# A three-block transformer kernel on one core: the order of the first modulation units in its head

## The reference

```python
def rmsnorm(x, g):
    y = xf * lax.rsqrt(jnp.mean(xf * xf, axis=-1, keepdims=True) + EPS)
    return (y * g).astype(x.dtype)

def ada_modulation(cond, w, b):
    m = jax.nn.silu(cond) @ w + b          # 1024 -> 6 * 1024
    return jnp.split(m, 6, axis=-1)        # shift, scale, gate, shift, scale, gate

def modulate(x, g, shift, scale):
    return rmsnorm(x, g) * (1 + scale[..., None, :]) + shift[..., None, :]

# first_block, layer 0
h  = modulate(x,  norm_mix[0], sh1,  sc1)       # 256 tokens
hc = modulate(xc, norm_mix[0], csh1, csc1)      # 256 context tokens
q, k, v, r = jnp.split(h @ w_in, ...)           # gated linear attention
z = ((h @ w1) @ w2 + b)                         # its gate, of rank 16
```

## Times and profile before

| | us |
|---|---|
| runs | 1339.34, 1339.40, 1344.83 |
| median | 1339.4 |
| the profiled execution | 1338.25 |
| its span | 1336.3 |
| PE busy | 1309.8 (98%) |
| ACT busy | 684.6 (51%) |
| DVE busy | 583.3 (44%) |
| POOL busy | 707.5 (53%) |
| read from HBM | 208.15 MB, 157 GB/s over the span |

### The profile page before, as it was taken

The page is one execution under the profiler, slowest core; times in us unless marked ns, Lnnn a source line. Parts: engine busy times, 40 slices in busy tenths (PEclk is TensorE's granted clock), DMA queues, the critical chain, the costliest instruction groups (busy, mean ns, idle before and its releaser), DMA issues.

```text
span 1336.3 us, 22359 instructions
## 1 busy us (share of the span) xinstructions
PE 1309.8 (98%) x8256; PEld 1105.9 (83%) x8256; DVE 583.3 (44%) x1105; ACT 684.6 (51%) x1056; POOL 707.5 (53%) x307
## 2 busy tenths in 40 slices
PE   5999999999999999999999999999999999999999
PEld 1688788777888888888777757999999987999999
DVE  3423686235444443400036465455532485556620
ACT  4561236344444444422137745666665667766652
POOL 0432002352544444454435211698899775798897
PEclk8999999999999999999999999999999999999999
DMA  9533733471333322353534351666666541566664
GB/s 358 189 95 95 265 130 142 157 273 58 111 98 101 99 94 94 126 204 98 170 137 142 95 205 52 230 196 194 191 202 209 177 139 61 192 198 193 189 206 126
DMA packets 60133, 210.19 MB, mean 157 GB/s; under 512 B 6432, under 2 KB 9760, under 8 KB 59936
## 3 DMA queue, kind: packets, MB, share of 16 engines
q1 hardware_dynamic: 59632, 207.52, 47.1%
q10 hardware_dynamic: 432, 1.70, 0.3%
HBM read 208.15 MB, written 1.05 MB: 157 GB/s over the span
## 4 chain that ended last, share of the span: by engine, by line
PE 94%; DVE 2%; ACT 1%; DMA 1%; SPq 1%; issue 1%; ACTq 0%; DVEq 0%
PE ps L351 74%; PE ps L478 2%; PE ps L1121 2%; PE ps L406 1%; PE ps L1115 1%; PE ps L1107 1%; PE ps L388 1%; PE ps L398 1%; PE ps L1478 1%; DMA raw<-wstream 1%; PE ps L1457 1%; SPq L313 1%; PE ps L1460 1%; PE ps L1101 1%; PE ps L1438 1%
## 5 line engine op out<-in xcount | busy, mean ns | idle before, releaser
L340 POOL TENSOR_TENSOR wlo<-raw,whi 128x1024 fp32r<-128x1024 f32 x291 | 695.2, 2406 | 613.6 <-ACT whi L335 612.8
L335 ACT ACTIVATE whi<-raw 128x1024 fp32r<-128x1024 f32 x291 | 306.5, 1056 | 214.2 <-PE ps L351 145.0
L351 PE MATMUL ps<-Hhi_,whi 128*128 128x256 f32 (+1 forms) x1336 | 388.6, 319 | 0.0
L351 PE MATMUL ps<-Hlo_,whi 128*128 128x256 f32 (+1 forms) x1336 | 384.6, 316 | 0.0
L351 PEld LDWEIGHTS ps<-Hhi_,whi 128*128 128x128 f32 x1336 | 250.9, 188 | 22.7 <-issue 4.6
L351 PEld LDWEIGHTS ps<-Hlo_,whi 128*128 128x128 f32 x1336 | 251.0, 188 | 19.9 <-issue 1.9
L351 PE MATMUL ps<-Hhi_,wlo 128*128 128x256 f32 (+1 forms) x1336 | 231.7, 316 | 0.0
L351 PEld LDWEIGHTS ps<-Hhi_,wlo 128*128 128x128 f32 x1336 | 194.4, 188 | 18.1
L351 PE MATMUL ps<-hidhi,whi 128*128 128x256 f32 (+1 forms) x528 | 151.1, 315 | 0.0
L351 PE MATMUL ps<-hidlo,whi 128*128 128x256 f32 (+1 forms) x528 | 150.7, 314 | 0.0
L774 ACT ACTIVATE u<-ps,par 128x256 f32<-128x256 f32 (+1 forms) x132 | 83.8, 635 | 114.5 <-PE ps L351 100.6
(11 more groups left out here) (331 smaller groups left out, 1605.1 us busy)
## 6 DMA issues: line engine op xcount, KB each, us to landing
raw<-wstream SPq DMA_DIRECT2D x367, 512.0 KB, 3.6
Haside_lo<-wstream SPq DMA_DIRECT2D x8, 512.0 KB, 5.7
Haside_hi<-wstream SPq DMA_DIRECT2D x8, 512.0 KB, 9.3
Paside<-wstream SPq DMA_DIRECT2D x4, 512.0 KB, 5.0
XT<-x_t SPq DMA_DIRECT2D x1, 1024.0 KB, 10.4
XT<-ctx_t SPq DMA_DIRECT2D x1, 1024.0 KB, 12.5
memx<-mem_t ACTq DMA_DIRECT2D x1, 1024.0 KB, 5.4
out_t<-XT SPq DMA_DIRECT2D x1, 640.0 KB, 6.2
```

The source lines that it names most:

```text
L335: nc.scalar.activation(whi[:, n % RING, :], raw[:, r % RAWS, :], ACT.Copy).then_inc(S["hi_ready"], 1)
L340: nc.gpsimd.tensor_tensor(wlo[:, r, :], raw[:, r, :], whi[:, n % RING, :].bitcast(F32), ALU.subtract).then_inc(S["lo_ready"], 1)
L351: mm = nc.tensor.matmul(o, a, b, start=start, stop=stop)
```

## The change

The first norm's modulation is made in two batches of another make-up: units 0 and 2 (shift and scale of rows 0 to 3), and units 1 and 3 (of rows 4 to 7). Unit 2 is loaded right behind unit 0. Unit 3 leaves the ring and is loaded into the buffer of v. The products of units 1 and 3 stand together behind row 3 of the first tiles, and ACT's copy of their batch ahead of row 4. Beside that, ACT's table set that has both logarithm and exponential is named once in the head, ahead of the squares.

```diff
-QUEUE = [unit(0, 0), unit(0, 1), unit(0, 2), ("gate", "gate", 0, 1), ("gq", "gq", 0, 1), unit(0, 3), ("gq_", "gq", 1, 3)] + whole("gk", "gv")
+QUEUE = [unit(0, 0), unit(0, 2), ("gate", "gate", 0, 1), ("gq", "gq", 0, 1), unit(0, 1), ("gq_", "gq", 1, 3)] + whole("gk", "gv")
...
-ASIDE = [2, 3, 6, 7, 11]
+ASIDE = [(0, 3), (1, 2), (1, 3), (1, 6), (1, 7), (1, 11)]
...
-for _early, _unit in (("gate", "mod0_3"),):
+for _early, _unit in (("gate", "mod0_1"),):
...
-                if k < 2 and norm == "mix0":
-                    mod_products(pe, 0, 3, (2 * k, 2 * k + 1))
-                if k == 2 and norm == "mix0":
+                if k == 3 and norm == "mix0":
+                    mod_products(pe, 0, 1)
+                    mod_products(pe, 0, 3)
                     mod_turn(pe, 1)
...
-        BATCHES = [(0, 0, 3), (0, 3, 4), (0, 4, 8), (0, 8, 12), (1, 0, 4), (1, 4, 8), (1, 8, 11), (1, 11, 12)]
+        BATCHES = [(0, (0, 2)), (0, (1, 3)), (0, (4, 5, 6, 7)), (0, (8, 9, 10, 11)), (1, (0, 1, 2, 3)), (1, (4, 5, 6, 7)), (1, (8, 9, 10)), (1, (11,))]
...
             mod_products(pe, 0, 0)
-            mod_products(pe, 0, 1)
             norm_pe(pe, "mix0", TT)
             mod_products(pe, 0, 2)
...
             act.wait_ge(S["xin"], 32)
+            nc.scalar.preload_act_table_set(LN_EXP)
             for m in range(KD):
...
-                if t == "mix0" and k == 3:
+                if t == "mix0" and k == 4:
                     mod_row(act, 1)
...
             for n in range(RAWS, RAWS + LATE):
+                if n == RAW["mod0_1"]:
+                    load_aside(sp, (0, 3))
                 load_slot(sp, n)
             sp.dma_start(glac[:, :], gla_c).then_inc(S["glac"], 16)
```

More of the change, by code:

```diff
@@ L88 @@
     SRC += range(HOST[_host] + _first, HOST[_host] + _first + _count)
-ASIDE = [2, 3, 6, 7, 11]
-ASIDE_LOADED = {2: 128, 3: 128, 6: 256, 7: 256, 11: 320}
+ASIDE = [(0, 3), (1, 2), (1, 3), (1, 6), (1, 7), (1, 11)]
+ASIDE_LOADED = {(0, 3): 64, (1, 2): 192, (1, 3): 192, (1, 6): 320, (1, 7): 320, (1, 11): 384}
 ASIDE_SLOT = {}
 for _u in ASIDE:
-    _name, _host, _first, _count = unit(1, _u)
+    _name, _host, _first, _count = unit(*_u)
     ASIDE_SLOT[_u] = HOST[_host] + _first
@@ L315, in load_aside @@
         def load_aside(sp, u):
-            if u in (2, 3):
+            if u in ((1, 2), (1, 3)):
                 sp.wait_ge(S["slot_used"], used(START["go"] - 1))
-            elif u in (6, 7):
+            elif u in ((1, 6), (1, 7)):
                 sp.wait_ge(S["slot_used"], used(START["dn0"] - 1))
-            else:
+            elif u == (1, 11):
                 sp.wait_ge(S["a_o"], MH)
@@ L326, in aside @@
         def aside(u):
-            return {2: Haside_lo, 6: Haside_lo, 3: Haside_hi, 7: Haside_hi, 11: Paside}[u]
+            return {(0, 3): gv, (1, 2): Haside_lo, (1, 6): Haside_lo, (1, 3): Haside_hi, (1, 7): Haside_hi, (1, 11): Paside}[u]
         def hi_slot(act, n, i=0):
@@ L451, in alink @@
             nc.scalar.wait_ge(S["act_step"], counters["a"])
-        BATCHES = [(0, 0, 3), (0, 3, 4), (0, 4, 8), (0, 8, 12), (1, 0, 4), (1, 4, 8), (1, 8, 11), (1, 11, 12)]
+        BATCHES = [(0, (0, 2)), (0, (1, 3)), (0, (4, 5, 6, 7)), (0, (8, 9, 10, 11)), (1, (0, 1, 2, 3)), (1, (4, 5, 6, 7)), (1, (8, 9, 10)), (1, (11,))]
         MOD_BANK = {0: 2, 1: 3, 2: 7, 3: 7, 4: 7, 5: 2, 6: 7, 7: 7}
         def batch_of(layer, u):
-            return next(i for i, (L, a, b) in enumerate(BATCHES) if L == layer and a <= u < b)
+            return next(i for i, (L, units) in enumerate(BATCHES) if L == layer and u in units)
         def mod_products(pe, layer, u, slots=range(MOD_UNIT)):
             v, batch = u % 4, batch_of(layer, u)
-            first, last = u == BATCHES[batch][1], u == BATCHES[batch][2] - 1
+            first, last = u == BATCHES[batch][1][0], u == BATCHES[batch][1][-1]
             if first and batch in (3, 4, 7):
@@ L467, in mod_products @@
             for s in slots:
-                if layer == 1 and u in ASIDE:
-                    pe.wait_ge(S["aside_in"], ASIDE_LOADED[u])
-                    rows, signal = aside(u)[:, s, :], S["aside_used"]
+                if (layer, u) in ASIDE:
+                    pe.wait_ge(S["aside_in"], ASIDE_LOADED[layer, u])
+                    rows, signal = aside((layer, u))[:, s, :], S["aside_used"]
                 else:
@@ L482, in mod_row @@
         def mod_row(act, batch):
-            layer, _, end = BATCHES[batch]
-            if layer == 1 and end - 1 in ASIDE:
-                act.wait_ge(S["aside_used"], MOD_UNIT * (ASIDE.index(end - 1) + 1))
+            layer, units = BATCHES[batch]
+            end = units[-1] + 1
+            if (layer, end - 1) in ASIDE:
+                act.wait_ge(S["aside_used"], MOD_UNIT * (ASIDE.index((layer, end - 1)) + 1))
             else:
@@ L502, in mod_bias @@
             dve.wait_ge(S["mod_tr"], batch + 1)
-            L, a, b = BATCHES[batch]
+            L, units = BATCHES[batch]
+            a, b = units[0], units[0] + 1 if batch < 2 else units[-1] + 1
             va, n = a % 4, b - a
@@ L661, in norm_act @@
             if t in ("ffn0", "mix1"):
-                act.wait_ge(S["aside_used"], MOD_UNIT * (ASIDE.index(UNIT_AFTER[t][0]) + 1))
+                act.wait_ge(S["aside_used"], MOD_UNIT * (ASIDE.index((1, UNIT_AFTER[t][0])) + 1))
             for i, (k, halves) in enumerate(norm_items(t)):
-                if t == "mix0" and k == 3:
+                if t == "mix0" and k == 4:
                     mod_row(act, 1)
@@ L2316, in _ @@
                 for u in ((2, 3), (6, 7), (11,), ())[part_]:
-                    load_aside(sp, u)
+                    load_aside(sp, (1, u))
             sync_tail(sp)
```

## The result

| | before | changed |
|---|---|---|
| runs, us | 1339.13 to 1344.83 | 1355.85 to 1357.87 |
| median | 1339.37 | 1356.54 |
| ratio, 95% interval | | 1.0125 (1.0105 to 1.0145) |
| the profiled execution | 1338.25 | 1357.15 |
| its span | 1336.3 | 1355.2 |

The changed kernel is slower by 17.2 us, inside the range given (1348.5 to 1357), 3.7 above the point forecast (+13.4).

The account below looks back on a forecast made before the run. It took a chain of waits in the head, then PE, without a gap from 52 to 130 us, as the bound. Terms 1.1 + 4.9 + 6.1 + 1.3 = 13.4 on the median 1339.4 gave 1352.8 us, range 1348.5 to 1357.

Parts of the forecast that it names:

- rival 1: Wait ahead of row 4: PE's clock falls a third time, costing 1.3 to 1.7, total 1354.3; chance 0.29.
- Term A: Head, up to the first row: PE wakes late at low clock, ACT copies batch 0 at 29.9; +1.1, from -0.2 to +2.7.
- 28.06: Head: forecast end of PE's low clock, 2.56 of work after the norm's sum starts at 25.50.
- Term B: Between rows 3 and 4: units 1 and 3 and the chain behind them stand in the open; +4.9, from 4.5 to 6.6.
- Term C: End of first tiles: `glac` and `w2` wait on SP's queue behind two blocked slots; +6.1, from +5.0 to +6.6.
- Term D: Behind the wait for `w2`: PE works 2.56 at half pace; +1.3, from 0.9 to 1.7.
- The removed loads: Eight table loads on ACT, 10.3 in all, said to bring nothing when removed.
- rival 3: ACT's table loads on the path: 1342.5, or 1331.5 with a drain per load; chance 0.02 each.
- the prediction's signs: Listed checks per term, among them last row's products ending at 56.5 and `w2` products starting at 62.8.

Follow-up runs that it names:

- e_tables_only: The kernel before with only ACT's table set named in the head, ahead of the squares; 1339.16 us, ratio 1.0003.
- e_unit2_ahead: The changed kernel with unit 2's products on PE ahead of the norm's sum, nothing else; 1352.34 us, ratio 1.0096.
- e_run_head: The changed kernel with 24 products of no use on PE between unit 0 and the norm's sum; 1353.56 us.
- e_glac_early: The changed kernel with glac and w2 issued by SP ahead of the two slots that wait for the first tiles; 1346.86 us, ratio 1.0055.
- e_spread: The changed kernel with unit 3 in place of three idle products ahead of row 0 and unit 1 halved into the steps of rows 0 and 1; 1351.74 us.
- e_run_rows: The changed kernel with 5 products of no use on PE behind the turn of units 1 and 3, ahead of row 4; 1354.2 us.
- e_run_tail: The changed kernel with 14 products of no use on PE ahead of its wait for w2; 1357.05 us.
- e_before_w2_late: The kernel before with glac and w2 issued by SP four slots later, behind slots 20 and 21; 1352.85 us, ratio 1.0091.
- e_best: The changed kernel with glac and w2 issued early, unit 2 ahead of the sum, units 1 and 3 spread, table set named before the input wait; 1341.42 us.
- e_best2: As e_best, but row 0 directly behind four idle products, unit 3 in row 0's step, unit 1 halved into those of rows 1 and 2; 1340.27 us.
- e_run_all: The changed kernel with products of no use in three PE gaps: 24 ahead of the sum, 5 ahead of row 4, 17 ahead of w2; 1352.75 us.

## Why the prediction was right, point by point

- **The direction and the range held**, the range partly by luck. All four terms are there, beside them only rival 1 came, and nothing behind 157 us moved. But the median stands 0.5 below the top of the range, and that top was made for rival 1 with the upper ends of A and C, while here D too went beyond its own (2.5 against 1.7). With the 18.9 of the profiled executions in place of the 17.2 of the medians, 1358.3, the result would lie above it.
- **Term A**, +1.1 forecast, +2.5 measured in the profiled execution. The mechanism is right (the moved load cancels but for 0.33 at most, by the first stage of e_tables_only; the late waking of PE is the cost, as e_unit2_ahead and e_run_head show). The step that was mis-sized is "28.06": the low clock did not end 2.56 after the start of work but 6.1 after it (to 31.5). In e_glac_early it ended at 28.5, with a first stage of 12.61, so +1.3; in the four kernels that keep this head (e_glac_early, e_spread, e_run_rows, e_run_tail) the stage was +1.3 to +1.6, near the forecast. The 2.7 given as the upper end was about the price of this execution. One record of a change is no price: before, it could have been read only that 2.56 is a length that occurred.
- **Term B**, +4.9 forecast, and +5.07 measured in the second stage, all of which e_spread gives back (17.9 in every other kernel that keeps the place, 13.1 in e_spread and in those built on the kernel before).
- **Rival 1**, the third fall of the clock, got 0.29 and 1.3 to 1.7. It came true in the profile, and cost 2.26, with 6.06 of work at 0.50. In e_glac_early, where that stage is 8.52, it cost 0.99. The argument against it, that gaps of 0.97 and 1.15 had left the clock alone, said nothing on one of 2.46; the row for a gap of 2.0 did, and should have weighed more. No gap length is a rule, though: one of 2.45 in e_run_head left the clock at 1.00.
- **Term C**, +6.1 forecast, +6.72 measured. SP's order was read rightly from the order of instructions. The first slot was there for ACT 3.6 after SP's signal (59.12 to 62.69), as forecast; the second slot and the small transfers behind it took 4.5 and not 3.9, which is the 0.6. In the other profiles with this wait the stage is 7.1 to 8.2 long, so 5.8 to 6.9 more than before, around the forecast.
- **Term D**, +1.3 forecast, +2.50 measured, up to 3.58 in e_before_w2_late. The same mis-sized step as in A: half of 5.3 of work at low clock, and not half of 2.56.
- **The removed loads** brought nothing, as forecast (e_tables_only), and rival 3 falls with them. On the drain that rival 3 priced: in the rows of e_tables_only the first square starts 0.01 after the load's end, so no drain is to be seen here either.

In the profiled execution the sum missed by 5.5 (18.9 and not 13.4): 1.4 in A, 2.3 by rival 1, 1.2 in D, so 4.9 of it by the clock, and 0.6 in C and 0.2 in B, less 0.1 for the earlier input. That execution is 0.6 above the median of its kernel and the one of before 1.1 below its own, so the medians show 3.7 of it. One number among the prediction's signs does not follow from its own sum: the last row's products end at 49.62 in the kernel before (49.01 + 0.61), and 6.0 later is 55.6, not 56.5. Nothing rests on it.

## What to carry to other kernels

A transfer that waits on an in-order queue holds up every one behind it: when the stream is re-ordered, ask for each small transfer behind it who is now released later, and issue constants ahead of the first slot that waits for late work. Work taken out of a gap of PE can cost twice, as here, once where it goes and once because the longer gap lets the clock fall; price the low clock from several profiles, not from one. A batch of products that was split over steps paced by DVE was free here (e_spread), as long as its weights had landed and the steps had room (e_best and e_best2 show where they had not); placed in one piece ahead of the step that needs it, it cost all of its time and the chain behind it.

## What was not expected of the hardware

How long PE stays at 1.2 GHz after work has begun differs by more than a factor of two: 2.6 us in the kernel before, 3.0 in the head of e_glac_early, 6.1 in that of the changed kernel, 7.6 behind the wait in e_before_w2_late. The same gap of 2.46 ahead of row 4 put the clock down for 6.1 of work in the changed kernel and for 3.5 in e_glac_early. And it can fall while PE is at work: 1.1 after row 4 had begun in e_glac_early, and 1.6 after a gap of 1.45 in e_run_tail. The stretches of e_glac_early from row 4 on:

```profile
47.94:48.90 0.96, 0.96 (x4) 0.83 (x5) 0.96 (x4) 0.28 (x1) 0.00 (x0) 1.00 0.00 0
49.00:52.40 3.40, 3.40 (x10) 2.55 (x9) 3.40 (x9) 1.95 (x6) 0.00 (x0) 0.51 0.00 0
```

Nor does the length of a gap tell whether the clock falls: in e_run_head it stayed at 1.00 through a gap of 2.45 and the work behind it, in e_run_all it fell 0.4 into the work behind one of 2.08. The stretches of e_run_head:

```profile
23.10:25.50 2.40, 0.00 (x0) 0.00 (x0) 2.08 (x3) 0.00 (x0) 0.00 (x0) 1.00 1.03 411
25.50:31.00 5.50, 5.46 (x34) 3.05 (x35) 0.51 (x3) 3.63 (x5) 0.77 (x1) 1.00 1.03 410
```

What decides it, and how long the low level lasts, no run here shows.
